# GLA gates of a hybrid diffusion step: computed between products of the gate path's projection instead of at the start of the scan

## The reference

```
h = rms_norm(x, g_pre) * (1 + scale) + shift
z = h @ w_in
a_q, a_k, a_v, b_q, b_k, b_v, c_q, c_k, c_v, c_lr, u = split(z)
g_f = log_sigmoid(c_lr[..., :16] @ c_w_f + c_b_f) / 16      # gates of the gated linear attention (GLA)
g_b = log_sigmoid(c_lr[..., 16:] @ c_w_b + c_b_b) / 16
o_a = attention(a_q, a_k, a_v); o_b = differential_attention(b_q, b_k, b_v)
o_c = gla_scan(c_q, c_k, c_v, g_f) + flip(gla_scan(flip(c_q), flip(c_k), flip(c_v), g_b))
y = (concat(o_a, o_b, o_c) * silu(u)) @ w_out
```

## Time and profile before

| | |
|---|---|
| median of 3 runs | 2391.35 us (2389.95 to 2392.23) |
| the profiled execution | 2391.01 us, its span 2389.1 us |
| busy, share of the span | TensorE 89%, VectorE 57%, GpSimd 41%, ScalarE 36% |
| projection, layer 1 | from about 58 us to 433 us; layer 2 ends at 1625 us |
| GLA, layer 1 | 433 us to 528 us |
| attention and output, layer 1 | 528 us to about 1230 us |

### The profile page before, as it was taken

One profiled execution on the slowest core, in us unless ns is written; L12 is line 12 of the kernel. 1 busy time (PEld: TensorE's weight loads), 2 busy tenths in 40 slices (PEclk: granted clock), 3 DMA queues, 4 the chain that ended last, 5 costly groups with the idle time before them and its releaser, 6 DMA issues. The chain is left out here.

```text
span 2389.1 us, 28515 instructions
## 1 busy us (share of the span) xinstructions
PE 2116.7 (89%) x10517; PEld 1478.5 (62%) x10517; DVE 1361.4 (57%) x2278; ACT 852.0 (36%) x1740; POOL 978.2 (41%) x522
## 2 busy tenths in 40 slices
PE   3799999889999999949938999998899999999498
PEld 1678888655555555528716789885555555555286
DVE  1667200596666666776516672005966666767764
ACT  2432221424445444432124322214244454444321
POOL 0211111325777777760002111113257777777500
PEclk9999999798999999969969999998999999999699
DMA  7332221110001010033373322211100010000333
GB/s 268 114 111 89 62 73 58 36 42 7 19 19 32 19 19 19 7 106 106 100 270 102 115 85 62 73 60 33 42 7 19 19 32 19 19 19 7 106 106 106
DMA packets 188756, 155.74 MB, mean 65 GB/s; under 512 B 125180, under 2 KB 150208, under 8 KB 186560
## 3 DMA queue, kind: packets, MB, share of 16 engines
q1 hardware_dynamic: 185424, 153.35, 21.2%
q10 hardware_dynamic: 3184, 0.47, 0.1%
HBM read 115.37 MB, written 38.42 MB: 64 GB/s over the span
## 5 line engine op out<-in xcount | busy, mean ns | idle before, releaser
L1150 POOL TENSOR_TENSOR prob_sums<-prob_sums,probs 128x1024 f32<-128x1024 f32 x256 | 614.4, 2400 | 108.9 <-ACT probs L1306 83.4
L1306 ACT ACTIVATE probs<-scores 128x512 f32<-128x512 f32 x672 | 361.5, 604 | 437.3 <-PE scores L1208 241.3
L501 POOL TENSOR_TENSOR w_lo<-w_stage,w_hi 128x512 fp32r<-128x512 f32 (+1 forms) x112 | 134.4, 1232 | 818.3 <-ACT w_hi L436 818.3
L1372 DVE TENSOR_REDUCE neg_max_parts<-work 128x1 f32<-128x512 f32 (+1 forms) x640 | 394.2, 683 | 60.5 <-PE work L1188 56.2
L403 PE MATMUL z_acc<-w_hi,h_hi 128*128 128x512 f32 (+1 forms) x640 | 237.0, 370 | 12.0 <-DVE h_lo L520 8.5
L403 PE MATMUL z_acc<-w_hi,h_lo 128*128 128x512 f32 (+1 forms) x640 | 234.2, 366 | 0.0
L403 PE MATMUL z_acc<-w_lo,h_hi 128*128 128x512 f32 (+1 forms) x640 | 234.0, 366 | 0.0
L1404 DVE RECIPROCAL recip_sums<-work 128x512 f32<-128x512 f32 x32 | 107.4, 3358 | 212.1 <-PE work L1240 212.1
L825 DVE MEMSET k_stackB<- 128x24 f32 (+1 forms) x4 | 0.9, 218 | 346.6 <-PEq L287 346.6
L403 PE MATMUL z_acc<-h_hi,w_lo 128*128 128x512 f32 (+1 forms) x528 | 187.0, 354 | 0.0
L403 PE MATMUL z_acc<-h_hi,w_hi 128*128 128x512 f32 (+1 forms) x528 | 186.9, 354 | 0.0
(11 more groups left out here) (230 smaller groups left out, 3734.8 us busy)
## 6 DMA issues: line engine op xcount, KB each, us to landing
w_stage<-in_w_in SPq DMA_DIRECT2D x96, 256.0 KB, 3.1
mod_w<-in_w_mod SPq DMA_DIRECT2D x16, 1024.0 KB, 14.1
z_scratch<-z_out SPq DMA_DIRECT2D x60, 256.0 KB, 2.0
cv<-u_scratch SPq DMA_DIRECT2D x20, 512.0 KB, 6.3
mod_w<-in_w_mod SPq DMA_DIRECT2D x16, 512.0 KB, 21.2
u_scratch<-z_out SPq DMA_DIRECT2D x32, 256.0 KB, 2.0
out_y_sample<-y_tiles SPq DMA_DIRECT2D x16, 512.0 KB, 5.1
q_rawA<-z_scratch SPq DMA_DIRECT2D x16, 320.0 KB, 4.0
```

The costliest lines, as they stand in the source:

```text
L501: pool.tensor_tensor(w_lo[:, n % RING, 0:cols], stage[:, n % STAGES, 0:cols], w_hi[:, n % RING, 0:cols].bitcast(F32), ALU.subtract).then_i ...
L1150: ins = pool.tensor_tensor(a, a, pr[:, n % NPB, :], ALU.add)
L1306: act.activation(pr[:, n % NPB, c * NB:(c + 1) * NB], sc[m % SCORE_BANKS][:, :], ACT.Exp, scale=SCALE[u]).then_inc(s["a_exp"], 1)
L1372: dve.tensor_reduce(dst, src, AX_X, ALU.max, negate=True).then_inc(s["a_wkdve"], 1)
```

## The change

The gates are computed inside the projection. The lr block moves ahead of the two u blocks, so that `lrT` is complete before them. Ahead of the third use of u TensorE computes the gate products of tiles 0 to 7, ahead of the seventh those of tiles 8 and 9, into the PSUM of the transposes `h_tr`, which is idle by then. ScalarE makes Abs, Exp and Ln behind the evacuation of these two uses, and VectorE finishes with one instruction for min and subtract. The gates lie in a tile `oc`, which is allocated once for the layer and holds, before, the z buffers `z_raw` and `z_tmp` of the projection (now two scratch parts where there were three), and after the GLA loop its output.

```
-BLOCKS = [("z", 2 * NB, NB), ("z", 0, NB), ("z", NB, NB), ("c", C_COL0, NB),
-          ("u", U_COL0, NB), ("u", U_COL0 + NB, NB), ("lr", LR_COL0, P)]
+BLOCKS = [("z", 2 * NB, NB), ("z", 0, NB), ("z", NB, NB), ("c", C_COL0, NB), ("lr", LR_COL0, P),
+          ("u", U_COL0, NB), ("u", U_COL0 + NB, NB)]
...
-        zt = sb("z_raw", [P, 3, NB])
+        oc5 = oc[:, :, :].rearrange("p (i t) c -> p i (t c)", t=2)
+        zt, tm = oc5[:, 0:3, :], oc5[:, 3:5, :]
         zo = sb("z_out", [P, 3, NB])
-        tm = sb("z_tmp", [P, 3, NB])
...
+        GATES_AT = U_USE0 + 2
+        pre = [tp[i // 2][:, (i % 2) * 4:(i % 2) * 4 + 4, :].rearrange("p k c -> p (k c)") for i in range(4)]
+        soft = [oc5[:, i, :] for i in range(T // 2)]
+        FIRST_GATES, LAST_GATES = range(4), range(4, T // 2)
...
+            def gate_products(groups):
+
+                pe.wait_ge(s["p_ev"], last_use[[kind for kind, _, _ in BLOCKS].index("lr")] + 1)
+                pe.wait_ge(s["p_h32"], T)
+                for i in groups:
+                    if i >= 4:
+                        pe.wait_ge(s["g_gate"], i - 3)
+                    for t in (2 * i, 2 * i + 1):
+                        mm = pe.matmul(pre[i % 4][:, (t % 2) * 2 * P:(t % 2 + 1) * 2 * P], per["lrT"][:, tile_rows(t)],
+                                       per["gate_w"][:, :], start=True, stop=True)
+                    mm.then_inc(s["g_pre"], 1)
...
+            def gate_softplus(groups):
+
+                act.wait_ge(s["p_zo"], Z_BLOCKS * T)
+                for i in groups:
+                    act.wait_ge(s["g_pre"], i + 1)
+                    act.activation(soft[i], pre[i % 4], ACT.Abs).then_inc(s["g_abs"], 1)
+                for i in groups:
+                    act.wait_ge(s["g_abs"], i + 1)
+                    act.activation(soft[i], soft[i], ACT.Exp, scale=-1.0).then_inc(s["g_sx"], 1)
+                for i in groups:
+                    act.wait_ge(s["g_sx"], i + 1)
+                    act.activation(soft[i], soft[i], ACT.Ln, bias=per["one"][:, :]).then_inc(s["g_ln"], 1)
...
+            for i in range(T // 2):
+                dve.wait_ge(s["g_ln"], i + 1)
+                dve.scalar_tensor_tensor(out=soft[i], in0=pre[i % 4], scalar=0.0, in1=soft[i], op0=ALU.min,
+                                         op1=ALU.subtract).then_inc(s["g_gate"], 1)
...
-        gate, soft = oa2[:, 0, :, :], oa2[:, 1, :, :]
+        gate = mid["oc"]
```

More of the change, by code:

```diff
@@ L282, in _, with projection_block @@
             do(dve.tensor_tensor(per["post"][:, :, :], mod[:, 1, :, :], both(bcols[:, NT + KD:], KD), ALU.mult))
-def projection_block(nc, l, io, per, f, s):
+def projection_block(nc, l, io, per, oc, f, s):
     with ExitStack() as ctx:
@@ L411, in _ @@
                 acc = zp[i % 4]
+                if i == GATES_AT:
+                    gate_products(FIRST_GATES)
+                elif i == GATES_AT + 4:
+                    gate_products(LAST_GATES)
                 if b == 0:
@@ L485, in _ @@
                 evacuate(i)
+                if i == GATES_AT:
+                    gate_softplus(FIRST_GATES)
+                elif i == GATES_AT + 4:
+                    gate_softplus(LAST_GATES)
                 if 0 < i <= Z_BLOCKS * T:
@@ L572, in finish_tile @@
                     if t < TS:
-                        do(dve.tensor_tensor(heads_view(tm[:, 2, 0:w], heads), heads_view(tm[:, 1, 0:w], heads), gain, ALU.mult))
-                        last = rope(o[:, 0:w], tm[:, 2, 0:w], t, heads, 16, per["cosA"], per["sinA"], tm[:, 1, 0:w])
+                        do(dve.tensor_tensor(zv, heads_view(tm[:, 1, 0:w], heads), gain, ALU.mult))
+                        last = rope(o[:, 0:w], z[:, 0:w], t, heads, 16, per["cosA"], per["sinA"], tm[:, 1, 0:w])
                     else:
@@ L626, in ps @@
             return ctx.enter_context(nc.psum_tensor(name, [P, NB], F32))
-        oa2 = mid["oa"][:, :, :].rearrange("p k t -> p (k t)").rearrange("p (x t c) -> p x t c", x=2, t=T)
         ob2 = mid["ob"][:, :, :, :].rearrange("p a k t -> p (a k t)").rearrange("p (x t c) -> p x t c", x=2, t=T)
-        gate, soft = oa2[:, 0, :, :], oa2[:, 1, :, :]
+        gate = mid["oc"]
         qt, oi = ob2[:, 0, :, :].rearrange("p t (d i) -> p t d i", d=2), ob2[:, 1, :, :]
@@ L683, in _ @@
             pe.transpose(tr_ps[0:2 * KD, 0:P], per["post"][:, :, :].rearrange("p g k -> p (g k)"), per["ident"][:, :]).then_inc(s["g_postT"], 1)
[L684 to L691, removed]
             def running_sums(t):
-                if t == 2:
-                    pe.wait_ge(s["g_gate"], 2)
                 if t >= 2:
@@ L775, in _ @@
             act.copy(post[:, :], tr_ps[0:2 * KD, 0:P]).then_inc(s["g_post"], 1)
[L776 to L784, removed]
             def exps(t):
@@ L827, in _ @@
             dve.memset(st[:, :, NC_S + 1, :], 0.0).then_inc(s["g_zero"], 1)
[L828 to L835, removed]
             def both(ap):
@@ L1764, in program @@
         with nc.Fori(0, DEPTH) as l:
+            whole = ctx.enter_context(ExitStack())
+            oc = whole.enter_context(nc.sbuf_tensor("oc", [P, T, C_HEADS * C_DV], F32))
             with ExitStack() as start:
@@ L1767, in program @@
                 modulation_block(nc, l, io, per, f, s)
-                projection_block(nc, l, io, per, f, s)
+                projection_block(nc, l, io, per, oc, f, s)
             with ExitStack() as branch:
                 mid = {n: branch.enter_context(nc.sbuf_tensor(n, shape, F32)) for n, shape in (
-                    ("oa", [P, A_HEADS * HEAD_DIM // P, TOK]), ("ob", [P, 2, B_HEADS * B_V // P, TOK]), ("oc", [P, T, C_HEADS * C_DV]))}
+                    ("oa", [P, A_HEADS * HEAD_DIM // P, TOK]), ("ob", [P, 2, B_HEADS * B_V // P, TOK]))}
+                mid["oc"] = oc
                 with ExitStack() as front:
```

## The result

The changed kernel took 2398.63 us (median of 17 runs, 2390.96 to 2404.27), the one before 2391.57 us in runs beside it (17, 2389.83 to 2394.41). The ratio is 1.0026, 95% interval 1.0019 to 1.0034: slower, by just over what can be told from no change. The forecast was +2.8 us, the measured difference is +7.1. The spread of single runs, from the shortest to the longest, grew from 4.6 to 13.3 us. The profiled execution took 2400.28 us, 9.3 us of span more than before.

A forecast was written before the change was run, and what follows sets the result against it. TensorE, busy 37.42 of 37.5 us, bounds the projection; a chain bounds GLA's start. Gate products 9.2 plus store 3.4 less GLA's gain 9.8 gave +2.8 us: 2394.2 us, range 2389.5 to 2399.0.

The forecast's parts named there:

- The bound and the places: TensorE bounds the projection, a chain GLA's start; costs in gate products and the last store, gain ahead of `blockdiag`.
- Rival 1: GLA's start: gates are the whole chain, GpSimd does not hold `blockdiag`; 27.2 us come off, 2376.8 us; chance 0.05.
- Rival 2: Projection: gate products cost TensorE nothing because u's products have slack; 2385.0 us; chance 0.05.
- Rival 3: Projection: u's weights come late behind the short lr block; 3.1 us per layer, 2400.4 us; chance 0.16.
- The range: Whole kernel: 2389.5 to 2399.0 us, holding the forecast and the mild part of the late-weights rival.
- the prediction's own limit of 2396.1: Whole kernel: above 2396.1 us counts as slower, below 2386.6 as faster; a 0.2% change, 4.8 us, is barely distinguishable.
- what TensorE pays in the projection: Between u's products: 20 gate-product records and their edges, 4.6 us per layer, 9.2 us in all.
- Its edges: Projection: switching between fp32 and rounded products at two insertions costs 0.1 to 0.6 us per layer, taken as 0.3.
- The store: Projection's end: u's last store, no longer hidden by lr, delays the barrier about 1.7 us per layer, 3.4 in all.
- GLA's start: First `blockdiag` comes earlier, held only by GpSimd's split: 5.0 us in layer 1, 4.8 to 4.9 in layer 2.
- Scaling q: GLA's start: VectorE's scaling could be slowed by GpSimd's split, delaying `blockdiag` some 0.5 us per layer; taken as nothing.
- The cold ramp of the score products: GLA: TensorE's clock returns some 5.1 us after the first score product, as before; 2 us either way is worth 1.

The follow-up runs named there:

- run 8: Changed kernel with GpSimd's split of unit A moved behind the `blockdiag` loop; 2392.27 us, ratio 0.9999 to the kernel before.
- run 1: Changed kernel with `lrT` and `gate_w` padded by zero weight rows, so gate products use 128 rows instead of 33; 2396.57 us, ratio 1.0022.
- run 4: Kernel before with only the lr block moved ahead of the two u blocks, gates still in GLA; 2398.36 us, ratio 1.0027.
- runs 1 to 3: run 1, and two more on the changed kernel: gate products spread as pairs over five products of u, 2399.32 us; every gate product issued twice, 2413.85 us.
- run 6: Changed kernel with the wait for u's last stores moved from the projection's end to the end of GLA's list on SyncE; 2398.76 us, ratio 1.0031.
- run 9: Changed kernel with unit A's three rounding copies on ScalarE and GpSimd's two subtractions behind the second `blockdiag`; 2385.09 us, ratio 0.9975.

## Why the prediction was right and wrong

- **The bound and the places: right.** All pieces of the sum stand where it put them, with their signs. Rival 1 fell to the split, as argued (run 8: it takes the split's move to get the early `blockdiag`). Rival 2 fell (run 1: 4.36 us for 20 records). Rival 3 fell for this order (run 4).
- **The range: held by luck.** 2398.63 us lies 0.4 below its upper end, above the 2391.5 to 2396.8 of the forecast itself. That part of the range was kept for late weights, which did not come; other things filled it. By the prediction's own limit of 2396.1 the result is "slower", to which it had given 0.23 and "same" 0.67.
- **The step that was mis-sized** is what TensorE pays in the projection, 4.6 us per layer. Its records, 20 x 0.216 = 4.3 us, are right at full clock. Its edges of 0.3 us are 0.41 to 0.43 per insertion, 0.85 per layer. And "at the clock that the projection has" took the clock for granted: in the run of eight it fell in some layers (+3.0 us, runs 1 to 3). That is 13.4 instead of 9.2 in the profiled execution. I had read the edge from transposes of 128 rows; with 128 rows the gates have next to none either (0.04 us per layer, run 1).
- **The store: right in kind, 0.3 too small per layer.** 2.0 instead of 1.7 us at the border; SyncE's wait is 1.3 us, and the issue of the store stands ahead of it (run 6: 0.6 us of the gap stay without the wait). The price that the prediction sets beside the row is, in the Trainium skill, "DMA: Bandwidth & Descriptors", section "Anatomy of one DMA — SWDGE (gpsimd) path", one for DMAs that GpSimd issues. These stores are issued by SyncE, so it does not price them, and no run here shows a store issued by GpSimd.
- **GLA's start: 4.4 and 4.2 instead of 5.0 and 4.8 to 4.9 us.** `blockdiag` follows the split as predicted. The split itself starts 448.83 - 443.09 = 5.74 us behind GLA's first copy instead of 438.44 - 433.43 = 5.01, since q's load took 4.9 us to landing instead of 4.1 (5.0 instead of 4.3 in layer 2). Scaling q was not caught by the split, as assumed: it ends at 446.67 + 0.42 = 447.09. The row behind that worry was misread, since VectorE's subtract ended at 446.61, 0.54 us behind the split and not with it; and the 17.5 us that it gives for the scaling of q before are 450.62 - 433.43 = 17.2 in its rows.
- **The sum with measured terms:** 2 x (4.32 + 0.85 + 2.0) - 8.6 = 5.7 us at full clock, and some 3.0 more with one fall. The median difference of 7.1 lies between 5.7 and 8.7. Falls that come in some executions only, and the late return of the clock at attention's start (2.6 us in the profiled one), widen the spread, but do not cover it: the shortest run, 0.6 us under the kernel before, is unexplained.
- **The cold ramp of the score products** (3.50 us for four records, 3.78 before) was assumed to be the same. In layer 1 the clock came back at 461.6 us, 3.1 behind the first score product, and before at 458.7, 5.2 behind it. By the prediction's own price for 2 us this is worth 1 us, and the table's last row shows -0.97 there. A ramp visibly shorter than 5 us was one of its own signs of being wrong.

## What to carry to other kernels

Work that is moved off a chain into a full stretch of another engine is paid in full there; what the chain gives back goes only to the next thing that stands in line, here GpSimd's split, so look for that before moving anything. Then the second move decides: the change alone lost 7 us, with the split out of the way it gained 6. Matmuls that contract over few rows, put between full ones, should be priced with their edges and with the clock behind them; zero rows up to 128 took away the edges, and no profile with them shows a fall.

## What the runs showed of the hardware

- TensorE's granted clock fell to 1.2 GHz while the engine was busy 1.00 of each stretch: inside a run of fp32 products of 33 rows, for about 6.8 us (335.3 to 342.1 us after), and again with each product issued twice, in both layers. With 128 rows none of six profiled layers shows a fall there.
- A run of 33-row products between full products costs 0.41 us per insertion beyond its records; with 128 rows 0.02.
- At the start of attention the clock came back late in four of 28 layers, which cost 2.6 us in the profiled execution after (granted clock 0.52 instead of 0.70 over 28 us).
- VectorE's updates of the states, with both tensor inputs in SBUF, took 3.27 us for two beside GpSimd's subtractions and 1.01 without (run 9). The two do not run side by side: each update ends 0.28 us behind the subtraction that it started beside (458.89 and 459.17, 460.57 and 460.85). The Trainium skill, "SBUF — State Buffer", section "SBUF: two separate sides", describes an exclusive lock between a VectorE instruction with two SBUF inputs and a GpSimd instruction that reads SBUF, held for a whole instruction, and the trace agrees (1.81 + 1.73 us of subtractions, 2.26 us added).
